# An MLP's high and low activations in one buffer, alternating in chunks of four sizes

## The reference

```python
def _sqrelu_mlp(h, w1, w2):
    return jnp.square(jax.nn.relu(h @ w1)) @ w2

def second_block(...):
    for i in range(DEPTH_2):              # 4
        h = _rmsnorm(x, norm_mix_g[i])
        ...                               # mixers: rglru, sgu, conv, rglru
        x = x + mix
        x = x + _sqrelu_mlp(_rmsnorm(x, norm_mlp_g[i]), mlp_w1[i], mlp_w2[i])
    return _rmsnorm(x, final_norm_g)
```

## Time and profile before

| | |
|---|---|
| runs | 2764.75, 2765.46, 2768.59 us |
| median | 2765.46 us |
| span of the profiled execution (first to last instruction) | 2766.9 us |
| TensorE matmuls busy | 2696.6 us, 97%, 19987 matmuls |
| weight loads busy | 2498.7 us, 90% |
| VectorE busy | 1782.1 us, 64% |
| ScalarE busy | 1212.4 us, 44% |
| GpSimd busy | 207.0 us, 7% |
| matmuls on `mh` and `ml` | 3 x 1024, first at 1849.8 us, last at 2756.4 us |

### The profile page before, as it was taken

How to read it: one execution, slowest core, us unless ns; L and a number is a source line. 1 busy time by engine, 2 the same in 40 slices (tenths; PEclk the granted TensorE clock), 3 DMA queues, 4 the chain that set the end, 5 groups by cost and what they waited for, 6 DMA issues and landing times. The chain is left out here.

```text
span 2766.9 us, 50426 instructions
## 1 busy us (share of the span) xinstructions
PE 2696.6 (97%) x19987; PEld 2498.7 (90%) x19987; DVE 1782.1 (64%) x2361; ACT 1212.4 (44%) x1802; POOL 207.0 (7%) x249
## 2 busy tenths in 40 slices
PE   7999999999999999999999999999999999999998
PEld 5888998798889988889879999999999999998998
DVE  4777535757772377742666558874676578668874
ACT  4332233643322332321555456554655446456553
POOL 1000012010000100000200014000300000004000
PEclk9999999999999999999999999999999999999999
DMA  6655523026653256542426543565556565653554
GB/s 248 199 187 191 164 90 102 16 80 202 185 192 103 84 168 189 185 143 99 132 80 206 198 158 108 175 200 195 206 178 202 178 204 177 202 178 108 183 199 136
DMA packets 153651, 444.74 MB, mean 161 GB/s; under 512 B 46512, under 2 KB 47920, under 8 KB 152880
## 3 DMA queue, kind: packets, MB, share of 16 engines
q1 hardware_dynamic: 119248, 431.38, 47.2%
q0 software_dynamic: 1120, 11.27, 1.1%
q10 hardware_dynamic: 33152, 0.26, 0.7%
HBM read 441.68 MB, written 1.18 MB: 160 GB/s over the span
## 5 line engine op out<-in xcount | busy, mean ns | idle before, releaser
L1875 DVE TENSOR_TENSOR wlo<-raw,whi 128x1024 fp32r<-128x1024 f32 x672 | 832.0, 1241 | 564.7 <-ACT whi L1336 562.1
L1336 ACT ACTIVATE whi<-raw 128x1024 fp32r<-128x1024 f32 x672 | 708.4, 1056 | 639.0 <-PE ps L589 578.7
L587 PE MATMUL ps<-nh,whi 128*128 128x512 f32 (+1 forms) x1491 | 538.2, 361 | 8.1 <-DVE nl L1948 6.7
L588 PE MATMUL ps<-nl,whi 128*128 128x512 f32 (+1 forms) x1491 | 529.4, 355 | 0.0
L589 PE MATMUL ps<-nh,wlo 128*128 128x512 f32 (+1 forms) x1491 | 529.3, 355 | 0.0
L587 PE MATMUL ps<-bh,whi 128*128 128x256 f32 x1456 | 404.4, 278 | 0.0
L588 PE MATMUL ps<-bl,whi 128*128 128x256 f32 x1456 | 403.1, 277 | 0.0
L589 PE MATMUL ps<-bh,wlo 128*128 128x256 f32 x1456 | 402.9, 277 | 0.0
L587 PEld LDWEIGHTS ps<-nh,whi 128*128 128x128 f32 x1491 | 281.9, 189 | 68.8 <-issue 13.8
L589 PEld LDWEIGHTS ps<-nh,wlo 128*128 128x128 f32 x1491 | 282.0, 189 | 39.8
L588 PEld LDWEIGHTS ps<-nl,whi 128*128 128x128 f32 x1491 | 282.2, 189 | 39.3 <-issue 0.5
(11 more groups left out here) (259 smaller groups left out, 4465.7 us busy)
## 6 DMA issues: line engine op xcount, KB each, us to landing
raw<-stream SPq DMA_DIRECT2D x800, 512.0 KB, 3.4
head<-stream SPq DMA_DIRECT2D x8, 1024.0 KB, 14.6
gates_w<-gate_in POOLq DMA_DIRECT2D x2, 3328.0 KB, 12.2
cst<-cst_in POOLq DMA_DIRECT2D x2, 1280.0 KB, 5.8
X<-x_in SPq DMA_DIRECT2D x1, 2048.0 KB, 8.0
out<-X SPq DMA_DIRECT2D x8, 128.0 KB, 2.0
fftw<-fftw_in POOLq DMA_DIRECT2D x2, 256.0 KB, 5.7
sbias<-sb_in POOLq DMA_DIRECT2D x1, 512.0 KB, 4.8
```

The source lines that it names most:

```text
L587: pe.matmul(dst, w1, rhs_hi, start=start, stop=False)
L588: pe.matmul(dst, w1, rhs_lo, start=False, stop=False)
L1336: act.activation(whi[:, at % RING, :], raw[:, n % RING, :], ACT.Copy).then_inc(w_hi_ready, 1)
L1875: dve.tensor_tensor(wlo[:, r, :], raw[:, PLACE["main", at] % RING, :], whi[:, r, :].bitcast(F32), ALU.subtract).then_inc(w_ready, 1)
```

## The change

The two buffers `mh` and `ml` become one, `mhl`, of the same total size and at the same place (64 modulo 256). A hidden tile of 256 tokens now takes 2048 bytes on a partition, in which chunks of the high part and of the low part take turns: 16 columns (64 bytes) each in the first MLP, 64 (256 bytes) in the second, 128 (512 bytes) in the third and 256 (1024 bytes) in the fourth. `part_of` gives the view of one part. Its users are TensorE's moving operand (`mlp_hid` in place of `hid`), ScalarE's write of the high part, and VectorE's subtraction, which reads the high part and writes the low part. The products and their order are the same, and every engine issues the same instructions in the same order; in each of the four up loops VectorE has one more instruction that computes an address, and in each of TensorE's down loops four address instructions are of another kind. ScalarE's write and VectorE's subtraction keep 512 columns per instruction, as 32 x 16, 8 x 64, 4 x 128 and 2 x 256. The first MLP's matmuls read 16 runs of 16 columns, the second's 4 of 64, the third's 2 of 128, the fourth's one run of 256.

```diff
--- before.py
+++ after.py
@@ -36,6 +36,7 @@
 LINES = 256
 WIDE_AT = 128
 NARROW_AT = 64
+MLP_CHUNK = [16, 64, 128, S]
 
 
 PLAN = [("ada_head", 16)]
@@ -326,8 +327,7 @@
         inv_row = sb("inv_row", [P, T])
         rstd_row = sb("rstd_row", [P, S])
         second = place[0]
-        mh = sb("mh", [P, NM * S], F32R, line=NARROW_AT)
-        ml = sb("ml", [P, NM * S], F32R, line=NARROW_AT)
+        mhl = sb("mhl", [P, 2 * NM * S], F32R, line=NARROW_AT)
 
         gates_at = (nc.sbuf_usable_end - 4 * 2 * len(GATE_BLOCKS) * P) // 32 * 32
         assert place[0] <= gates_at and hidden_s_end <= gates_at
@@ -482,6 +482,10 @@
                 return ps[:, 1:3, 0:S] if u == 0 else halved(ps[:, 3, :])
             return halved(ps[:, u % 2, :])
 
+        def part_of(cols, i, part):
+
+            return cols.rearrange("p (a b c) -> p a b c", b=2, c=MLP_CHUNK[i])[:, :, part, :]
+
         def halved(row):
 
             return row.rearrange("p (a t) -> p a t", a=2)
@@ -939,6 +943,13 @@
                     return buf[:, bass.ds(kdyn * (4 * step) + (base + k * step), w)]
                 return at
 
+            def mlp_hid(i, part):
+                def at(k, kdyn):
+                    if isinstance(kdyn, int):
+                        return part_of(mhl[:, k * T:(k + 1) * T], i, part)
+                    return part_of(mhl[:, bass.ds(kdyn * (4 * T) + k * T, T)], i, part)
+                return at
+
             def short_down(name, w, src_h, src_l, order, readies, free=None):
 
 
@@ -1317,7 +1328,7 @@
                 else:
                     conv(i)
                 mlp_up(f"mlp_up{i}")
-                down(f"mlp_down{i}", NM, S, hid(mh, S, S), hid(ml, S, S), 2)
+                down(f"mlp_down{i}", NM, S, mlp_hid(i, 0), mlp_hid(i, 1), 2)
             norm((0, 0, 0), split=False)
 
 
@@ -1451,7 +1462,6 @@
                 act.wait_ge(up_evac, udyn + (u + 1))
                 if mlp:
                     act.activation(halved(tmpa[:, u % 2, :]), up_pair(local, first), ACT.Relu).then_inc(up_act, 1)
-                    w, dst = T, mh
                 else:
                     act.activation(tmpa[:, u % 2, 0:w], bank(2 * (u % 2), w), ACT.Silu).then_inc(up_act, 1)
                     dst = hh if w == T else hs_both
@@ -1459,6 +1469,12 @@
                     between()
 
                 act.wait_ge(up_evac, udyn + (u + 3))
+                if mlp:
+                    chunk = MLP_CHUNK[c["mlp"]]
+                    act.activation(part_of(mhl[:, bass.ds(ldyn * 2 * T + local * 2 * T, 2 * T)], c["mlp"], 0),
+                                   tmpb[:, u % 2, :].rearrange("p (a c) -> p a c", c=chunk),
+                                   ACT.Copy).then_inc(hid_hi, 1)
+                    return
                 act.activation(dst[:, bass.ds(ldyn * w + local * w, w)], tmpb[:, u % 2, 0:w],
                                ACT.Copy).then_inc(hid_hi, 1)
 
@@ -1850,6 +1866,7 @@
                 upper_gain(lambda m, i=i: ("norm_mlp", i * KD + m), in_h)
                 c["rms"] += 1
                 mlp_up(f"mlp_up{i}")
+                c["mlp"] += 1
                 down(f"mlp_down{i}", NM)
 
             act.wait_ge(sq_added, c["sb"])
@@ -2090,8 +2107,14 @@
             def hidden_lower(u, udyn, w, mlp, local, ldyn):
 
                 if mlp:
-                    w, h, l_ = T, mh, ml
-                elif w == T:
+                    chunk = MLP_CHUNK[c["mlp"]]
+                    both = mhl[:, bass.ds(ldyn * 2 * T + local * 2 * T, 2 * T)]
+                    dve.wait_ge(hid_hi, udyn + (u + 1))
+                    dve.tensor_tensor(part_of(both, c["mlp"], 1),
+                                      tmpb[:, u % 2, :].rearrange("p (a c) -> p a c", c=chunk),
+                                      part_of(both, c["mlp"], 0).bitcast(F32), ALU.subtract).then_inc(hid_lo, 1)
+                    return
+                if w == T:
                     h, l_ = hh, hl
                 else:
                     h = l_ = hs_both
```

## The result

The changed kernel takes 2774.03 us (median of ten runs, 2772.05 to 2774.94). The kernel before, run beside it on the same chip, takes 2767.15 us (ten runs, 2764.72 to 2768.59). The ratio is 1.0024 with a 95% interval of 1.0015 to 1.0032: slower by 6.9 us, a quarter of a per cent. The prediction had 2766 us and "no change" as its likeliest case. The measured time is outside the 2761 to 2771 us of that case. It lies inside the whole range only because that was drawn up to 2787 us to let in Rival 1, and it falls between the two prices of Rival 1, 2771 and 2786 us, in the MLP that Rival 1 named.

What follows compares the result with a forecast made beforehand. TensorE was taken to bound the kernel, busy 97% of the span and without waits in the down stages. All terms were 0, summing to 0 on 2766.9 us; forecast 2766 us, range 2761 to 2787 us.

Steps and rivals of the forecast that it cites:

- no change: Whole kernel: the change costs nothing, 2766 us, own range 2761 to 2771 us; chance 0.47.
- Rival 1: In MLP 0, TensorE's activation and weight reads clash by quarters: 20.5 us, 2786 us in full; chance 0.34.
- The bound: Down stages: TensorE never idles, so their length is matmul count times start-to-start distance, 768 x 113.3 ns, 87.0 us each.
- MLPs 1 to 3: the term of 0: TensorE's down stages in MLPs 1 to 3: shifted starts and jumps between pieces cost 0.
- ScalarE and VectorE: the terms of 0: Up stages: ScalarE's write (633 ns) and VectorE's subtraction (684 ns) cost 0, any lengthening fitting into idle time.
- Rival 4: VectorE's write in 64-byte pieces takes three times as long or more: about 2771 us; chance 0.03.
- this step: TensorE in MLP 0's down stage: cost 0, as two matmuls of three keep their start at 64.
- more likely error: MLP 0's down stage: only the low part, starting at 128, pays 6.7 ns per matmul, 1.7 us.
- 0 to 5.1 us: MLP 0's down stage: cost allowed by the nearest row, contiguous reads from 128 at 120 ns.
- The sign set for this: Profile after, MLP 0's down stage: starts 120 to 140 ns apart would bear the clash of TensorE's two reads.
- small case: MLP 0: the two reads meet once per matmul, 5.1 us, 2771 us; chance 0.04.
- Rivals 2 and 3: Rival 2: MLP 0's gaps read along, 216 ns, 2845 us, 0.07; 3: faster matmuls, 2761 or 2745 us, chance 0.09.

Runs made afterwards that it cites:

- the jumps experiment: Kernel before, down stages reading 64-byte pieces in steps of 128, 128 (from 128), 320 and 256 bytes: 120.0, 120.02, 113.35, 120.01 ns; 2783.01 us.
- the last probe: Kernel before, down stages reading 64-, 128-, 32- and 64-byte pieces in steps of 192, 256, 64 and 320 bytes: 117.78, 119.99, 118.34, 119.98 ns; 2782.59 us.
- the first undoing: Changed kernel with 256-byte chunks in the first MLP too: 2774.43 us, ratio 1.0022; repeated on another chip 2768.17 us, ratio 1.0003.

## Why the prediction was wrong where it was

**The bound was right.** TensorE has no idle time in the down stages, before or after, and the result is pace times count: 768 x 7.1 ns = 5.47 us in MLP 0.

**MLPs 1 to 3: the term of 0 was right.** 113.4 ns against 113.3. That "the jumps keep the address modulo 256" was the reason given; the third row of the jumps experiment shows the stronger form, that jumps that only keep the order of the quarters are free too.

**ScalarE and VectorE: the terms of 0 were right.** 633 and 684 ns, and VectorE's idle time of 1.06 to 1.10 us per unit unchanged. Rival 4 is out.

**MLP 0: this step failed.** "I take 0, since the high parts (two matmuls of three) keep their start": measured 5.47 us. The reason given was the mistake. It takes the start for the thing that costs, when the rows at 113.3 and 120 ns were of contiguous reads, in which the start fixes the quarter of every later column. With gaps it does not. In the jumps experiment the read from 64 in steps of 128 pays 6.7 ns by itself, and in the changed kernel L591 and L593, which read the high part, are as slow as L592. The "more likely error" of 1.7 us, which let only the low part pay, fails for the same reason. The end of "0 to 5.1 us", from the row at 120 ns for all three matmuls, was nearly the measured value. The sign set for this, 120 to 140 ns in MLP 0, came with 120.45 ns; the other, a down stage longer by more than 5.5 us, fell short by 0.03 us. That 2774 us lies in the range is luck: neither the term of 0 nor the main price of Rival 1 was the right size, and the time fell between them.

**Rival 1 had the right pair of reads and mis-sized the cost.** The shifted weights show that the place of the moving read against the weights sets the cost, in quarters of 256 bytes, as it said. Its picture of meetings had starts at 0 and 192 as free as 64, and they were not. Its main price, four meetings of 6.7 ns each and 2786 us, did not come: in most orders the cost is about one quarter's worth, 6.7 to 7.1 ns, with two pieces to a 256-byte line or one, and in two orders of the last probe it is 4.4 and 5.0 ns. Its small case, one meeting and 2771 us, lies nearest to the measured 2774; it had 0.04 of the chance. Counting meetings is thus not how the cost adds up; why it stops at about 7 ns isn't shown.

**Rivals 2 and 3 are out.** No order of reads came near 216 ns, or below 113.3.

**The rule of the Trainium skill** ("SBUF — State Buffer", Specifications), by which pieces of four 16-byte hits a line are free, does not decide here: pieces of 64 bytes ran at 120.45 ns in MLP 0 and at 113.35 in steps of 320 bytes. What the runs show has a step of 64 bytes and a period of 256, relative to the weights.

**What stays open.** Why starts at 0 and 192 are no cheaper; why the cost has a ceiling; what sets a stage off at 113.4 or at 117.8 ns; whether the 117.78 ns from 192 is that second pace; the high times of the first undoing. No version tried beat the kernel before.

## What to carry to other kernels

When two moving operands of TensorE are interleaved in one buffer, make the piece a multiple of 256 bytes, so that both keep a start that is cheap against the weights (here 64 against 128 modulo 256), or step so that the 64-byte quarters are passed in the order of a contiguous read; in a stretch that TensorE bounds, the other orders tried cost 4 to 6% of the pace here. Do not judge a strided read by where it starts: a row of a contiguous read speaks only for reads that pass the same places in the same order. After any move of buffers, read the distance between starts stage by stage, also in stages that were not touched.

## What was not expected of the hardware

- The pace of a matmul with 256 fp32 columns takes few values: 113.35, 117.8 and 120.0 to 120.5 ns in nearly every probe (118.34 once). It moves by a quarter of 256 bytes in the weights as it does by one in the moving operand.
- At the same addresses, 113.4 and 117.8 ns both last through a whole down stage of 768 matmuls.
- With 512 columns the good start is another one: nh at 128 gives 226.9 ns and at 64 gives 233.3 ns, while with 256 columns it is 120 and 113 to 114.
- Writes of ScalarE and VectorE in pieces of 64 bytes cost nothing (633 and 684 ns).
